# A mixture-of-experts gather of 96 partitions issued over 128, with the slots of a tile laid in blocks of 32 over both halves of the partitions

## The chip, the core and the metric

The kernel runs on one NeuronCore of a Trainium2 chip. The metric is the device time of one execution in microseconds; the time before is the median of three runs. The engines named below are TensorE (PE), VectorE (DVE), ScalarE (ACT), GpSimd (POOL) and SyncE (SP). SP issues the loads of the weights, ACT issues stores, POOL issues gathers (indirect DMAs); all of them are carried out by the core's 16 DMA engines. Everything is float32.

## The reference

Two layers of a diffusion trunk over 256 latent and 256 context tokens of width 1024. A layer is a mixer and then a mixture of experts. What matters here is the mixture of layer 0, over all 512 tokens:

```python
g_logits = (x @ w_group).astype(jnp.float32) + b_group          # top-1 of 4 groups
...
top_p, top_i = lax.top_k(e_prob, MOE_TOP_K)                      # top-2 of the group's 4 experts
...
for e in range(MOE_EXPERTS):                                     # 16 experts, hidden width 512
    hdn = jax.nn.silu(x @ w_gate[e]) * (x @ w_up[e])
    y = y + combine[:, e:e + 1] * (hdn @ w_down[e])
```

An expert has three matrices of 2 MB. Each of the 512 tokens goes to two experts, so that 1024 rows are shared among 16 experts, 64 on average. With the reference's inputs the router (worked out from the inputs, not from a trace) gives, in the order in which the kernel takes its tiles (experts 15 to 2, then 0, then 1, whose last 10 tokens make a seventeenth, narrow tile): 86, 92, 79, 49, 87, 76, 63, 64, 15, 34, 51, 50, 81, 37, 54, 96 and 10 tokens. Layer 1 does the same for the 256 latent tokens, 32 rows to an expert on average; there the experts have 5, 30, 34, 25, 19, 34, 14, 35, 36, 59, 37, 56, 60, 39, 12 and 17 tokens.

## The kernel before

Each engine has its own hand-written program, and the programs wait for each other on semaphores. The experts of a layer are done one after the other, a tile of at most `CAP[0] = 96` token rows each in layer 0 (`CAP[1] = 64` in layer 1). A tile is called by its place e below, 0 to 16; its buffers are the pair p = e % 2.

**Weights.** SP loads blocks of 2 MB (gate, up and down of every expert, written `ring<-in_moe_w_gate` and so on in the trace) into a ring of 6 slots. `block_used` counts the blocks that PE is done with, and SP issues a load when its slot is free (L586 in the loop, L540 outside it). PE waits for a block with `pe.wait_ge(arrival(i), ...)` at the head of `gate_up` and `down`.

**Which token sits in which slot.** `router` runs on DVE. From the rank of a token among those of its expert it makes `sl`, the slot in the tile, and `tile`. For tiles 0 and 1 a quick way is taken: `first_hot` compares a row of slot numbers (`count_row`) with the places of the tokens (L2088), PE multiplies the result with the token numbers (bank `FIRST_IDX_BANK`), and DVE writes the indices `idx` (L2112). For all tiles DVE makes `slot_hot` (a comparison of `sl` with 0 to 127, L2133) and `tile_hot` (L2140, L2142), PE multiplies them (16 matmuls), and DVE writes `idx` again (L2154). A slot without a token gets an index beyond the bounds, and the gather skips it.

**Gathers.** `gather` on POOL copies one column of `idx` (L2760), and `rows_in` issues the indirect DMA (L2768 for layer 0, L2771 for layer 1): partition s of `xg` gets the row of `h2_rows` in HBM that is token idx[s], 4 KB in layer 0. In layer 1 a token takes two partitions, s and 64 + s, with 2 KB each. From tile 2 on the gather of tile e waits until DVE has turned the rows of tile e - 2 (`xgT_dve`). The first tile is turned by PE (`first_xt`, L1183), the others by DVE in blocks of 32 partitions (`do_rows_turned`, L2261).

**Products.** PE takes the slots in three groups of 32 as stationary operand against the weights (`do_product`, matmuls at L638 and L1089), then `do_down`. Nothing in them depends on which token is in which slot.

**Results.** DVE and ACT copy the down product into `yb`, and ACT stores it by two DMAs (`store_y`, L451 and L452) into `y_rows` in HBM, at row tile * 96 + slot. POOL fetches each token's two rows again by `y_gather` (L2808): four gathers of 128 rows after tile 13 is stored (`y_gathered_early`), four more after tile 14, four after tile 15. Their positions `py` come from `tile` and `sl` as well (L2146). The sum over the two experts is then added to the residual and normed, and layer 1 begins.

Of the kernel before, what the change touches and what calls it, by code (L numbers as in the profile page):

```python
# [13 lines left out]
P = 128  # L14
D = 1024
KC = D // P
NT = 4
# [146 lines left out]
def hybrid_dit(nc, A, out):  # L164
# [4 lines left out]
    with ctx:  # L169
# [123 lines left out]
        pick = hidT[:, 0, 2, :].rearrange("p (j n) -> p j n", j=NLAT)  # L293
        count_row, place = hidT[:, 0, 3, 0:CAP[0]], hidT[:, 1, 3, 0:2 * NT]
        first_hot = view(M_HID, 2, NT * CAP[0])
        key_hit = yb[:, :, 512:1024]
# [339 lines left out]
        def _(pe):  # L636
            def mm(o, l, r, start=True, stop=True):
                return nc.tensor.matmul(o, l, r, start=start, stop=stop)  # L638
# [358 lines left out]
            def rows_and_router(l):  # L997
# [59 lines left out]
                if l == 1:  # L1057
                    keep_clock(0, (512, 256))
                    pe.wait_ge(sem("h2_act"), NT + NLAT)
                    first_picked()  # L1060
                else:
                    for e in range(2):
                        pe.wait_ge(sem("picked"), e + 1)
                        for j in range(NT):
                            m = mm(ps[0:CAP[0], FIRST_IDX_BANK[e], 0:1], first_hot[:, e, j * CAP[0]:(j + 1) * CAP[0]],
                                   cst[:, C_TOK + j:C_TOK + j + 1], j == 0, j == NT - 1)
                        m.then_inc(sem("idx_ps"), 1)
                    pe.wait_ge(sem("h2_act"), NT)
                    ada_block(4, 3)
# [817 lines left out]
        def _(dve):  # L1887
# [109 lines left out]
            def router(l):  # L1997
# [33 lines left out]

                V.tensor_scalar(count_row[:, 0:CAP[l]], ps[:, 1, 384:384 + CAP[l]], 1.0, None, ALU.add)
                link(V.tensor_reduce(r("gm"), lgv[:, :, 0:4], AX_X, ALU.max))
# [52 lines left out]
                for e in range(2 - l):  # L2086
                    hot = pick if l == 1 else first_hot[:, e, :].rearrange("p (j n) -> p j n", j=NT)
                    V.tensor_tensor(hot, count_row[:, 0:cap].unsqueeze(1).to_broadcast([P, n, cap]),  # L2088
                                    place_of[:, e if l else 1 - e, :].unsqueeze(2).to_broadcast([P, n, cap]), ALU.is_equal)\
                        .then_inc(sem("picked"), 1)  # L2090
# [6 lines left out]
                if l == 0:  # L2097
# [12 lines left out]
                    for e in range(2):  # L2110
                        dve.wait_ge(sem("idx_ps"), e + 1)
                        V.tensor_scalar(idx[0:cap, e:e + 1], ps[0:cap, FIRST_IDX_BANK[e], 0:1], float(NO_TOKEN), None, ALU.add)\  # L2112
                            .then_inc(sem("idx_ready"), 1)
# [12 lines left out]
                if l == 0:  # L2126
                    V.tensor_tensor(r12("sl"), r12("sl"), r12("pb"), ALU.add)
                link(V.tensor_tensor(r12("tile"), r12("xk"), r12("ke"), ALU.add))

                th = tile_hot[:, 0:2 * n * NTL].rearrange("p (t k) -> p t k", t=2 * n)  # L2130
# [546 lines left out]
        def _(pool):  # L2677
# [74 lines left out]
            def gather(l, e, p):  # L2752
# [3 lines left out]
                if not (isinstance(e, int) and e < 2):  # L2756
                    pool.wait_ge(sem("xgT_dve"), EB[l] + e - 1 - l)
                ex = e if isinstance(e, int) else bass.ds(e, 1)
                rows = CAP[0] if l == 0 else P
                G.tensor_copy(idxc[0:rows, p:p + 1], idx[0:rows, e:e + 1] if isinstance(e, int) else idx[0:rows, ex])\  # L2760
                    .then_inc(sem("idx_col"), 1)
# [4 lines left out]
            def rows_in(l, b):  # L2766
                if l == 0:
                    return G.indirect_dma_start(xg[0:CAP[0], b, :], None, h2_rows,  # L2768
                                                bass.IndirectOffsetOnAxis(ap=idxc[0:CAP[0], b:b + 1], axis=0),
                                                bounds_check=NT * P - 1, oob_is_err=False)  # L2770
# [154 lines left out]
```

## Time and profile before

| | us |
|---|---|
| runs before, median of 3 | 1002.42 |
| lowest and highest of the 3 | 1001.57 and 1005.04 |
| the profiled execution, its own time | 999.99 |
| its span, from the first to the last instruction | 998.2 |
| PE busy | 944.5 (95%) |
| DVE busy | 622.6 (62%) |
| ACT busy | 182.3 (18%) |
| POOL busy | 116.2 (12%) |

The span is what the trace shows; 1.8 us of the execution's own time lie around it. A busy PE is not a PE at its peak, and a short wait in it can be the whole of what a transfer costs. Layer 0's mixture runs from about 315 to 625 us of the span, layer 1's from about 760 us to the end.

### The profile page before, as it was taken

The numbers are of one execution on the slowest core, as the hardware profiler recorded it, in microseconds if no ns is written. First come the engines' busy times: TensorE is split into PE (matmuls) and PEld (weight loads), VectorE is DVE, ScalarE is ACT, GpSimd is POOL, SyncE is SP. The second block draws the span as 40 slices with busy tenths as digits, with TensorE's granted clock in tenths as the row PEclk, the third lists the DMA queues.
The fourth block names the chain that finished last, engine by engine and source line by source line (L and its number), as shares of the span: only waits on it lengthen the run. The fifth ranks groups of instructions, "written<-read, shape, count | busy, mean of one in ns | idle before, by whom it ended". The sixth has DMA issues, their size and how long they took to land.

```text
span 998.2 us, 19918 instructions
## 1 busy us (share of the span) xinstructions
PE 944.5 (95%) x8010; PEld 569.0 (57%) x8010; DVE 622.6 (62%) x1527; ACT 182.3 (18%) x343; POOL 116.2 (12%) x176
## 2 busy tenths in 40 slices
PE   5999999999998999999999998999998899999986
PEld 2443433456445788988888894445644455555542
DVE  2100799879546696676866645647416977777763
ACT  3010022255024010000000003317503100000001
POOL 7010100101400200000001214100010100000000
PEclk9999999999999699999999999999999999999998
DMA  9999967456836899999999967945125899999993
GB/s 315 372 417 414 373 232 273 140 200 254 237 120 238 291 361 346 399 410 415 402 410 398 425 264 276 367 166 197 62 88 193 316 428 423 427 424 427 426 427 153
DMA packets 55758, 312.01 MB, mean 313 GB/s; under 512 B 7137, under 2 KB 17121, under 8 KB 38288
## 3 DMA queue, kind: packets, MB, share of 16 engines
q1 hardware_dynamic: 41152, 277.88, 70.3%
q0 software_dynamic: 9376, 21.20, 6.7%
q10 hardware_dynamic: 5168, 12.06, 3.2%
q8 instruction: 45, 0.74, 0.3%
q14 instruction: 17, 0.14, 0.0%
HBM read 300.52 MB, written 17.25 MB: 318 GB/s over the span
## 4 chain that ended last, share of the span: by engine, by line
PE 78%; DMA 9%; DVE 7%; issue 2%; ACT 1%; POOL 1%; SPq 1%; ACTq 0%; POOLq 0%; DVEq 0%
PE ps L638 52%; PE ps L1089 10%; DMA ring<-in_moe_w_gate 5%; PE ps L653 3%; PE ps L982 3%; PE ps L1222 2%; PE ps L1132 2%; DMA ring<-in_ada_w 2%; DMA ar<-y_rows,sm 1%; PE ps L1477 1%; DMA y_rows<-ar 1%; SPq L536 1%; PE ps L918 1%; PE ps L663 1%; PE ps L1446 1%
## 5 line engine op out<-in xcount | busy, mean ns | idle before, releaser
L638 PE MATMUL ps<-ring,ar 128*32 128x384 f32 (+6 forms) x3872 | 475.1, 464 | 7.8 <-DMA ring<-in_moe_w_gate 4.6
L638 PEld LDWEIGHTS ps<-ring,ar 128*32 128x32 f32 (+2 forms) x3872 | 196.1, 120 | 133.0 <-issue 75.2
L1089 PE MATMUL ps<-ring,ar 128*32 128x128 f32 x1488 | 167.4, 275 | 0.0
L1089 PEld LDWEIGHTS ps<-ring,ar 128*32 128x32 f32 x1488 | 163.8, 111 | 2.8
L2261 DVE STREAM_TRANSPOSE ar<-ar 32x256 f32<-32x256 f32 x304 | 132.3, 435 | 4.5
L638 PE MATMUL ps<-xh,ring 128*128 128x512 f32 x256 | 114.0, 598 | 1.4 <-ACT xh L1526 1.4
L2303 DVE TENSOR_TENSOR ar<-ar,ps 128x384 f32<-128x384 f32 (+2 forms) x33 | 15.9, 482 | 119.4 <-PE ps L1089 68.2
L638 PE MATMUL ps<-ring,xh 128*128 128x512 f32 x192 | 86.3, 605 | 2.3 <-ACT xh L1537 1.4
L638 PEld LDWEIGHTS ps<-xh,ring 128*128 128x128 f32 x256 | 47.5, 190 | 62.6 <-issue 60.4
L2432 DVE SCALAR_TENSOR_TENSOR ar<-ar,cpar 128x512 f32<-128x512 f32 x120 | 79.6, 747 | 0.0
L1597 ACT ACTIVATE ar<-ps 128x384 f32<-128x384 f32 (+2 forms) x33 | 14.3, 432 | 275.7 <-PE ps L638 192.0
L638 PEld LDWEIGHTS ps<-ring,xh 128*128 128x128 f32 x192 | 36.4, 193 | 49.0 <-issue 45.2
L2290 DVE STREAM_TRANSPOSE ar<-ar 32x64 f32<-32x64 f32 x256 | 60.5, 236 | 4.5
L2282 DVE STREAM_TRANSPOSE ar<-ar 32x128 f32<-32x128 f32 x144 | 59.5, 413 | 2.9
L1132 PE MATMUL ps<-ring,ar 128*32 128x256 f32 x256 | 57.9, 379 | 0.0
L2760 POOL COPY sm<-sm 96x1 int32 (+3 forms) x32 | 6.0, 189 | 325.1 <-DVE ar L2261 309.6
L653 PE MATMUL ps<-ring,silu_c 128*32 128x512 f32 x320 | 40.1, 619 | 0.0
L2400 DVE TENSOR_TENSOR ar<-ps,gm 128x512 f32<-128x512 f32 x12 | 8.3, 690 | 50.8 <-PE ps L638 39.7
L1132 PEld LDWEIGHTS ps<-ring,ar 128*32 128x32 f32 x256 | 28.1, 110 | 18.0
L1602 ACT ACTIVATE ar<-ps 128x512 f32<-128x512 f32 x16 | 9.6, 598 | 150.2 <-PE ps L638 150.2
L2421 DVE TENSOR_TENSOR ar<-ps,ar 128x512 f32<-128x512 f32 x4 | 2.8, 693 | 43.5 <-PE ps L638 43.5
L1222 PE MATMUL ps<-ar 64*128 64x512 f32 x120 | 29.8, 615 | 0.0
(398 smaller groups left out, 946.6 us busy)
## 6 DMA issues: line engine op xcount, KB each, us to landing
ring<-in_moe_w_gate SPq DMA_DIRECT2D x31, 2048.0 KB, 16.4
ring<-in_moe_w_up SPq DMA_DIRECT2D x30, 2048.0 KB, 15.6
ring<-in_moe_w_down SPq DMA_DIRECT2D x30, 2048.0 KB, 17.8
ring<-in_ada_w SPq DMA_DIRECT2D x24, 2048.0 KB, 13.6
ring<-in_even_w_in SPq DMA_DIRECT2D x4, 2048.0 KB, 14.8
y_rows<-ar POOLq DMA_DIRECT2D x17, 384.0 KB, 10.2
ring<-in_odd_w_in SPq DMA_DIRECT2D x3, 2048.0 KB, 19.4
y_rows<-ar ACTq DMA_DIRECT2D x16, 288.0 KB, 8.9
```

Source lines behind the costliest of these rows:

```text
L638: return nc.tensor.matmul(o, l, r, start=start, stop=stop)
L653: m = nc.tensor.matmul(ps[32 * q:32 * q + 32, LATE_BANK if g == 4 and n >= 2 else ADA_BANK[g], :], silu_c[:, 2 * k + c, 10 - 2 * s:42 - 2 ...
L982: m = nc.tensor.matmul(ps[:, j, :], mix[:, c, j * P:(j + 1) * P], blk(i)[:, c, :], start=(c == 4), stop=(c == 3), skip_group_check=True)
L1089: m = nc.tensor.matmul(ps[96:128, bank, g * P:(g + 1) * P], xgT[:, p, c, 32 * g:32 * g + 32], w[:, c, 3 * P:HID], start=c == 0 and g == 0, ...
L1132: nc.tensor.matmul(ps[96:128, 5, 256 * g:256 * g + 256], tokens(g, c), w[:, c, 768:D], start=c == 0 and g == 0, stop=c == HC - 1 and g == ...
L1222: m = nc.tensor.matmul(acc(j, h), mixw[64 * h:64 * h + 64, p, j * P:(j + 1) * P], yb[64 * h:64 * h + 64, p, 0:512], start=False, stop=True ...
L1597: A_(hid[:, p, 0:hw], ps[:, 0, 0:hw], ACT.Silu).then_inc(sem("silu_done"), 1)
L2261: m = V.transpose(xgT[32 * q:32 * q + 32, p, :, slots], rows)
L2282: V.transpose(hidT[32 * q:32 * q + 32, p, :, 32 * r:32 * r + 32], cols[:, q, :, :])
L2290: m = V.transpose(hidT[32 * q:32 * q + 32, p, 0:2, 32 * r:32 * r + 32], cols[:, q, :, :])
L2303: V.tensor_tensor(hid[:, p, 0:hw], hid[:, p, 0:hw], ps[:, 1, 0:hw], ALU.mult).then_inc(sem("hid_ready"), 1)
L2432: V.scalar_tensor_tensor(acc[n], u_in[:, n, :, bass.ds(t, 256)], cpar[:, n, bass.ds(t, 1)], acc[n], ALU.mult, ALU.add).then_inc(sem("conv_ ...
```

## The change

Layer 0's gathers are issued over all 128 partitions of `xg` instead of 96. Slots 0 to 31 stay on partitions 0 to 31, slots 32 to 63 go to partitions 64 to 95, slots 64 to 95 to partitions 32 to 63; the last 32 partitions have no token and are skipped. For tiles 0 and 1 the new order comes from a permuted `count_row`, with `first_hot` 128 instead of 96 wide; for the others from four more DVE operations on `sl` (add 32 from slot 32 on, take 64 away from slot 64 on). `py` follows `sl`, so the rows of `y_rows` are permuted within a tile too.

```diff
@@ -291,8 +291,8 @@
         slot_of, half_of = (tile_hot[:, half + NTL + k:half + NTL + k + 1] for k in (8, 9))
         mixw = hid[:, :, 256:512]
         pick = hidT[:, 0, 2, :].rearrange("p (j n) -> p j n", j=NLAT)
-        count_row, place = hidT[:, 0, 3, 0:CAP[0]], hidT[:, 1, 3, 0:2 * NT]
-        first_hot = view(M_HID, 2, NT * CAP[0])
+        count_row, place = hidT[:, 0, 3, :], hidT[:, 1, 3, 0:2 * NT]
+        first_hot = view(M_HID, 2, NT * P)
         key_hit = yb[:, :, 512:1024]
         posy, posy_early = sm[:, 16:24].bitcast(I32), sm[:, 8:16].bitcast(I32)
         EARLY = NEXP - 2
@@ -1062,7 +1062,7 @@
                     for e in range(2):
                         pe.wait_ge(sem("picked"), e + 1)
                         for j in range(NT):
-                            m = mm(ps[0:CAP[0], FIRST_IDX_BANK[e], 0:1], first_hot[:, e, j * CAP[0]:(j + 1) * CAP[0]],
+                            m = mm(ps[:, FIRST_IDX_BANK[e], 0:1], first_hot[:, e, j * P:(j + 1) * P],
                                    cst[:, C_TOK + j:C_TOK + j + 1], j == 0, j == NT - 1)
                         m.then_inc(sem("idx_ps"), 1)
                     pe.wait_ge(sem("h2_act"), NT)
@@ -2029,7 +2029,9 @@
                 link(V.tensor_tensor(lgv, ps[:, 1, 0:32 * n].rearrange("p (j k) -> p j k", k=32)[:, :, 0:20],
                                      r_bias.unsqueeze(1).to_broadcast([P, n, 20]), ALU.add))
 
-                V.tensor_scalar(count_row[:, 0:CAP[l]], ps[:, 1, 384:384 + CAP[l]], 1.0, None, ALU.add)
+                V.tensor_scalar(count_row[:, :].rearrange("p (a b s) -> p a b s", a=2, b=2) if l == 0 else count_row[:, 0:CAP[1]],
+                                ps[:, 1, 384:512].rearrange("p (b a s) -> p a b s", a=2, b=2) if l == 0
+                                else ps[:, 1, 384:384 + CAP[1]], 1.0, None, ALU.add)
                 link(V.tensor_reduce(r("gm"), lgv[:, :, 0:4], AX_X, ALU.max))
                 V.tensor_tensor(r4("ge"), lgv[:, :, 0:4], b4("gm"), ALU.subtract).then_inc(sem("g_shift"), 1)
                 link(V.tensor_tensor(r4("eq"), lgv[:, :, 0:4], b4("gm"), ALU.is_equal))
@@ -2085,8 +2087,9 @@
                                             ALU.add, ALU.mult))
                 for e in range(2 - l):
                     hot = pick if l == 1 else first_hot[:, e, :].rearrange("p (j n) -> p j n", j=NT)
-                    V.tensor_tensor(hot, count_row[:, 0:cap].unsqueeze(1).to_broadcast([P, n, cap]),
-                                    place_of[:, e if l else 1 - e, :].unsqueeze(2).to_broadcast([P, n, cap]), ALU.is_equal)\
+                    wide = CAP[1] if l else P
+                    V.tensor_tensor(hot, count_row[:, 0:wide].unsqueeze(1).to_broadcast([P, n, wide]),
+                                    place_of[:, e if l else 1 - e, :].unsqueeze(2).to_broadcast([P, n, wide]), ALU.is_equal)\
                         .then_inc(sem("picked"), 1)
                 ranks = ranks.unsqueeze(1).to_broadcast([P, 2, n, 16])
                 V.tensor_tensor(r32("t12"), r32("M12"), ranks, ALU.mult)
@@ -2109,7 +2112,7 @@
                                            ALU.mult, ALU.add)
                     for e in range(2):
                         dve.wait_ge(sem("idx_ps"), e + 1)
-                        V.tensor_scalar(idx[0:cap, e:e + 1], ps[0:cap, FIRST_IDX_BANK[e], 0:1], float(NO_TOKEN), None, ALU.add)\
+                        V.tensor_scalar(idx[:, e:e + 1], ps[:, FIRST_IDX_BANK[e], 0:1], float(NO_TOKEN), None, ALU.add)\
                             .then_inc(sem("idx_ready"), 1)
 
                 V.tensor_tensor(r32("t12"), r32("lower"), over_experts(nov), ALU.mult)
@@ -2124,8 +2127,13 @@
                 link(V.tensor_tensor(r12("xk"), r12("xk"), r12("ne"), ALU.add))
                 link(V.scalar_tensor_tensor(r12("xk"), r12("kk"), 0.0, r12("xk"), ALU.is_gt, ALU.mult))
                 if l == 0:
-                    V.tensor_tensor(r12("sl"), r12("sl"), r12("pb"), ALU.add)
+                    link(V.tensor_tensor(r12("sl"), r12("sl"), r12("pb"), ALU.add))
                 link(V.tensor_tensor(r12("tile"), r12("xk"), r12("ke"), ALU.add))
+                if l == 0:
+                    V.tensor_scalar(r12("pb"), r12("sl"), 32.0, 32.0, ALU.is_ge, ALU.mult)
+                    link(V.tensor_scalar(r12("q"), r12("sl"), 64.0, -64.0, ALU.is_ge, ALU.mult))
+                    link(V.tensor_tensor(r12("pb"), r12("pb"), r12("q"), ALU.add))
+                    link(V.tensor_tensor(r12("sl"), r12("sl"), r12("pb"), ALU.add))
 
                 th = tile_hot[:, 0:2 * n * NTL].rearrange("p (t k) -> p t k", t=2 * n)
                 th4 = tile_hot[:, 0:2 * n * NTL].rearrange("p (k j t) -> p k j t", k=2, t=NTL)
@@ -2756,8 +2764,7 @@
                 if not (isinstance(e, int) and e < 2):
                     pool.wait_ge(sem("xgT_dve"), EB[l] + e - 1 - l)
                 ex = e if isinstance(e, int) else bass.ds(e, 1)
-                rows = CAP[0] if l == 0 else P
-                G.tensor_copy(idxc[0:rows, p:p + 1], idx[0:rows, e:e + 1] if isinstance(e, int) else idx[0:rows, ex])\
+                G.tensor_copy(idxc[:, p:p + 1], idx[:, e:e + 1] if isinstance(e, int) else idx[:, ex])\
                     .then_inc(sem("idx_col"), 1)
                 pool.wait_ge(sem("idx_col"), EB[l] + e + 1 - l)
                 pool.sem_inc(sem("waits_passed"), 1)
@@ -2765,8 +2772,8 @@
 
             def rows_in(l, b):
                 if l == 0:
-                    return G.indirect_dma_start(xg[0:CAP[0], b, :], None, h2_rows,
-                                                bass.IndirectOffsetOnAxis(ap=idxc[0:CAP[0], b:b + 1], axis=0),
+                    return G.indirect_dma_start(xg[:, b, :], None, h2_rows,
+                                                bass.IndirectOffsetOnAxis(ap=idxc[:, b:b + 1], axis=0),
                                                 bounds_check=NT * P - 1, oob_is_err=False)
                 return G.indirect_dma_start(xg[:, b, 0:512], None, h2_halves,
                                             bass.IndirectOffsetOnAxis(ap=idxc[:, b:b + 1], axis=0),
```

On DVE, in layer 0's `router`, between the last sums that give slot and tile and the comparison that makes `slot_hot` (128x1024), there stood before (all names are of the one buffer `ar`; `ps` is PSUM):

```order
L2125 SCALAR_TENSOR_TENSOR ar<-ar 128x8 [waits dve_chain]
L2127 TENSOR_TENSOR ar<-ar 128x8 [waits dve_chain]
L2128 TENSOR_TENSOR ar<-ar 128x8
L2133 TENSOR_TENSOR ar<-ps,ar 128x1024 [waits dve_chain]
L2140 TENSOR_TENSOR ar<-ps,ar 128x256
L2142 TENSOR_TENSOR ar<-ar,cst 128x256 [waits dve_chain]
```

At the same place of the changed kernel (its lines are numbered 8 higher from here on):

```order
L2130 TENSOR_TENSOR ar<-ar 128x8 [waits dve_chain]
L2131 TENSOR_TENSOR ar<-ar 128x8 [waits dve_chain]
L2133 TENSOR_SCALAR ar<-ar 128x8 [waits dve_chain]
L2134 TENSOR_SCALAR ar<-ar 128x8
L2135 TENSOR_TENSOR ar<-ar 128x8 [waits dve_chain]
L2136 TENSOR_TENSOR ar<-ar 128x8 [waits dve_chain]
L2141 TENSOR_TENSOR ar<-ps,ar 128x1024 [waits dve_chain]
L2148 TENSOR_TENSOR ar<-ps,ar 128x256
L2150 TENSOR_TENSOR ar<-ar,cst 128x256 [waits dve_chain]
```

Four operations of 8 elements have come in, three of them waiting for the one before, and one wait more stands ahead of the sum for `tile` (L2131). The two comparisons for tiles 0 and 1, further ahead on DVE, are 128x512 instead of 128x384.

On POOL, at the start of layer 0's dispatch, the clearing of `xg`, and the first two gathers before:

```order
L2747 MEMSET ar 128x2048 [waits chosen,y_zero]
L2760 COPY sm<-sm 96x1 [waits h2_stored0,h2_stored1,idx_ready,pool_chain]
L2768 DMA ar<-h_rows,sm 96x1024 [waits idx_col]
L2760 COPY sm<-sm 96x1 [waits idx_ready]
L2768 DMA ar<-h_rows,sm 96x1024 [waits idx_col]
```

and of the changed kernel:

```order
L2755 MEMSET ar 128x2048 [waits chosen,y_zero]
L2767 COPY sm<-sm 128x1 [waits h2_stored0,h2_stored1,idx_ready,pool_chain]
L2775 DMA ar<-h_rows,sm 128x1024 [waits idx_col]
L2767 COPY sm<-sm 128x1 [waits idx_ready]
L2775 DMA ar<-h_rows,sm 128x1024 [waits idx_col]
```

No order and no wait has moved there; the copy and the gather are wider. PE, ACT and SP keep their rows, but for the 8 one-column matmuls of tiles 0 and 1, which give 128 rows instead of 96.

## Rows read from the trace of the kernel before

**Rows 1.** The page: the chain that ended last, share of the span by engine.
```profile
PE 78%; DMA 9%; DVE 7%; issue 2%; ACT 1%; POOL 1%; SPq 1%; ACTq 0%; POOLq 0%; DVEq 0%
```

**Rows 2.** Windows of layer 0's tiles: us, busy time, PEclk, DMA share, GB/s.
```profile
381.70:397.40 15.70, 15.70 (x270) 13.48 (x264) 11.07 (x27) 1.09 (x2) 1.15 (x2) 1.00 0.90 326
...
444.30:538.30 94.00, 93.69 (x1578) 80.64 (x1571) 65.58 (x157) 6.52 (x12) 6.95 (x12) 1.00 1.01 406
```

**Rows 3.** Waits between 320 and 620 us: total, times, longest.
```profile
PE ps L638 <- DMA ring<-in_moe_w_gate: 2.1, 1, 2.1
...
PE ps L638 <- DMA ring<-in_moe_w_down: 0.3, 1, 0.3
```

**Rows 4.** The chain that ended last, 500 to 630 us: start, us, what.
```profile
514.21 28.37 DMA ring<-in_moe_w_gate
...
591.27 7.25 DMA y_rows<-ar
...
599.31 0.99 POOL xh L2808
...
613.37 10.49 DMA ar<-y_rows,sm
```

**Rows 5.** Layer 0's last two weight loads: SP's timeline, and their landing.
```profile
558.84 5.57 SPq L540 DMA_DIRECT2D ring<-in_moe_w_down  x2
...
DMA to landing us min/median/max: 25.1/25.3/25.4
```

**Rows 6.** Windows at the end of layer 0's and of layer 1's weights (columns as rows 2).
```profile
568.00:576.00 8.00, 8.00 (x130) 6.03 (x129) 6.42 (x16) 0.60 (x1) 2.84 (x2) 1.00 1.01 423
576.00:580.00 4.00, 4.00 (x81) 4.00 (x74) 1.11 (x3) 0.39 (x1) 0.00 (x0) 1.00 0.98 416
580.00:584.00 4.00, 4.00 (x82) 4.00 (x74) 0.00 (x0) 0.10 (x1) 0.00 (x0) 1.00 0.73 304
584.00:589.20 5.20, 5.20 (x81) 4.33 (x76) 4.14 (x10) 0.00 (x0) 0.23 (x1) 1.00 0.32 130
976.00:980.00 4.00, 3.70 (x26) 1.59 (x24) 2.08 (x9) 0.00 (x0) 0.00 (x0) 1.00 0.88 354
980.00:983.00 3.00, 2.35 (x12) 0.63 (x10) 2.86 (x11) 0.00 (x0) 0.00 (x0) 1.00 0.19 78
```

**Rows 7.** DVE's timeline in layer 0's router.
```profile
322.13 1.03 DVE L2088 TENSOR_TENSOR ar<-ar 128x384 f32<-128x384 f32 x2
...
327.56 0.17 DVE L2125 SCALAR_TENSOR_TENSOR ar<-ar 128x8 f32<-128x8 f32 x1
327.76 0.17 DVE L2127 TENSOR_TENSOR ar<-ar 128x8 f32<-128x8 f32 x1
327.85 0.16 DVE L2128 TENSOR_TENSOR ar<-ar 128x8 f32<-128x8 f32 x1
328.04 1.23 DVE L2133 TENSOR_TENSOR ar<-ps,ar 128x1024 f32<-128x1024 f32 x1
```

**Rows 8.** PE's timeline there; idle time before it and its releaser in brackets.
```profile
330.11 3.62 PE L638 MATMUL ps<-ar 128*128 128x32 f32 x16 [1.08 <-DVE ar L2142]
333.55 1.52 PE L1183 MATMUL ps<-cst,ar 96*128 96x96 f32 x8
```

**Rows 9.** Layer 0's first gather, the landing of its 17, and layer 1's gathers (128 wide).
```profile
327.62 1.03 POOL L2768 DMA_INDIRECT ar<-h_rows,sm  x1 [0.98 <-POOL sm L2760]
...
DMA to landing us min/median/max: 4.6/10.4/10.9
...
L2771 POOL DMA_INDIRECT ar<-h_rows,sm x15: 1013/1019/1077, 776.7 to 933.4; - x15
```

**Rows 10.** Window about the first tile (columns as rows 2).
```profile
330.00:340.70 10.70, 9.80 (x71) 9.01 (x75) 5.16 (x27) 1.77 (x2) 2.07 (x3) 0.50 1.02 354
```

**Rows 11.** The second store of tile 13 and the first early gather: timelines of ACT and POOL.
```profile
575.70 0.45 ACTq L452 DMA_DIRECT2D y_rows<-ar  x1
...
588.97 1.09 POOL L2808 DMA_INDIRECT xh<-y_rows,sm  x1 [18.07 <-DMA y_rows<-ar]
```

## Prediction

> **What bounds the kernel now.** I read the page first. The chain that ended last is PE for 78% of the span and DMA for 9% [rows 1], so anything done to a gather counts only where PE stands still for it, where its transfer is itself on the chain, or where it takes DMA time from what is. The second view is the windows over layer 0's tiles. Tile after tile PE is busy 15.7 of 15.7 us, while the 16 DMA engines are busy too: the share is 0.90 about tiles 2 and 3 and 1.01 from tile 6 to 12 [rows 2]. Two resources are nearly even here, and a few tenths of a microsecond per tile decide which is ahead. The third view says who is: of 320 to 620 us PE waits once for a gate block, 2.1 us, and once for a down block, 0.3 us [rows 3]. The chain has the first of them: a gate block is issued at 514.21 and lands 28.37 us later, at 542.58, where PE had arrived at 542.58 - 2.1 = 540.5 [rows 4]. For twelve tiles PE has lived on the lead of the ring, and at 540 it is used up.
>
> The fourth view shows what kind of lateness that is. The last load of layer 0 is issued at 558.84 + 5.57 - 0.33 = 564.1 and lands 25.1 us later, at 589.2 [rows 5]. All 16 engines should be busy until then. They are not: the share is 0.98, then 0.73, then 0.32 in the last 5.2 us [rows 6]. Some engines have done their part long before the slowest, and a block counts as landed only when the slowest has. The unused engine time is 4 x 0.02 + 4 x 0.27 + 5.2 x 0.68 = 4.7 us per engine: the slowest engine is 4.7 us behind the mean. The weight blocks are alike for all engines, so it is the rows of the gathers (4 KB, whole rows per engine) that are laid unevenly. At the end of layer 1, whose gathers fill both halves of the partitions, the same sum is 4 x 0.12 + 3 x 0.81 = 2.9 us [rows 6].
>
> **What the change does to the DMA engines.** At 423 GB/s over 16 engines [rows 6] a row of 4 KB costs an engine 4096 / 26,400 = 0.155 us. Backlog builds up from tile 6 on (before it the share is below 1, and a light engine simply idles). Tiles 6 to 15 have 63, 64, 15, 34, 51, 50, 81, 37, 54 and 96 tokens, 545 in all, 34 per engine. Two ways of dealing partitions to engines fit the 4.7 us of before. (a) Eight engines serve partitions 0 to 63, each two blocks of four (0-3 and 32-35, and so on), eight serve 64 to 127: the heaviest gets 8 rows of a tile of 64, in sum 74, that is 40 above the mean or 6.2 us. (b) Consecutive partitions, six per engine: the heaviest gets 60, 26 above, 4.0 us. Layer 1 tells them apart for gathers of 128: with its tokens on s and 64 + s, in rows of 2 KB (0.078 us), (a) gives a heaviest engine of 95 rows against a mean of 64, 2.4 us; eight consecutive partitions per engine give 125 rows, 4.7 us. Measured are 2.9, nearer to (a). I take (a). After the change slots 0 to 31 then fall on the first eight engines, 32 to 63 on the other eight, and only tokens beyond 64 go back to the first: the heaviest engine gets 4 rows of a tile, 8 of one above 67, in sum 48, 14 above the mean or 2.2 us. So the slowest engine is earlier at 542 by 4.7 - 2.2 = 2.5 us, by (a) alone 26 x 0.155 = 4.0 us. I take 3, and keep 0.8 as the lower bound: layer 1's 2.9 us over 15 tiles of half-size rows, scaled to 10 tiles of whole ones, is 3.9 us, only 0.8 less than 4.7.
>
> The Trainium skill says the same of the deal in "DMA: Bandwidth & Descriptors", section "The descriptor swizzle": a 128-partition transfer is dealt by fours, engines 0 to 7 for partitions 0 to 63. By that rule, the trace of layer 1 agrees (2.9 us beside 2.4). The same page, section "Why a DMA increments its semaphore by 16 and not by 1", speaks against the change: it counts a 96-partition tile among those that use all 16 engines, six partitions each. By that reading before is case (b), 60 rows against 48 after: 12 x 0.155 = 1.9 us instead of 3, and PE would still wait a few tenths.
>
> **What it costs ahead of the first tile.** Four operations of 8 elements come in on DVE ahead of the comparison for `slot_hot`, and one wait more. A pair with a wait between is 0.20 us apart, one without 0.09 (327.56, 327.76, 327.85) [rows 7]: 3 x 0.20 + 0.09 for the four, and 0.11 for the wait, 0.8 us. The two comparisons of tiles 0 and 1 go from 384 to 512 columns: they take 0.52 each, and 1024 columns 1.23, so 1.1 ns a column, 2 x 128 x 1.1 = 0.28 us [rows 7]. Together 1.1 us. This lies on the chain: PE waits 1.08 us for L2142 before the 16 index matmuls at 330.11, and runs the first tile's turn right behind them at 333.7 [rows 8]. The first gather stays covered: issued at 327.62, landed 4.6 us later at 332.2, 1.5 us before it is needed [rows 9]; it moves by only the 0.28. POOL's issue of a gather costs 1.03 us and a 128-wide one of layer 1 1.019, nothing to add [rows 9]. PE's granted clock is 0.50 through 330 to 340.7 [rows 10]; 1.1 us of delay can cost between 0.6 (the clock rises at the same moment, and the work pushed behind it runs at twice the rate) and 2.6 (it rises some 3 us late). I take 1.1. Later gathers have a whole tile of 15.7 us for landings of 10.4 [rows 2, 9], and DVE, busy 11 of 15.7, turns blocks of 32 partitions as before.
>
> **The sum.** PE arrives at the critical block at 540.5 + 1.1 - 0.3 (the down wait, gone) = 541.3. The block, pushed by 1.1 as well since its stream is paced by PE until about tile 6, lands at 542.58 + 1.1 - 3 = 540.7. The wait is gone, and PE goes on at 541.3 instead of 542.6: -1.3 us. What follows runs at PE's pace: per tile the heaviest engine has 6.3 MB / 16 of weights, a store of 0.39 MB / 16 and 4.8 rows, 0.44 MB at 26.4 GB/s, 16.6 us, where before it had 7.4 rows and 17.0; that is more than 15.7, so a little of the gain is eaten again, but only three tiles are left.
>
> At the end of the layer the stores are on the chain. POOL's first early gather starts at 588.97, when tile 13's store has landed, 13.3 us after its issue at 575.70 [rows 11]: that store shares the engines with the last weights, and the slowest engine is the one that holds 4.7 us more. Even engines end at 589.2 - 2.5 = 586.7 or before, so the four early gathers (1.3 us apart) start 1 to 2.5 us earlier, and tile 14's store, issued at 591.27 in the midst of them and landed 7.25 us later [rows 4], meets less of them. POOL's next gathers (599.31) wait for it. Beyond the 1.3 us that everything moves I count 1.0 more here (bounds 0 and 3). From there to the end all is released by layer 0's results, and moves along. Sum: -1.3 - 1.0 = -2.3 us on the profiled execution, 999.99 to 997.7. The runs lie higher (median 1002.42); the same difference gives 1000.1.
>
> **Rivals.** (A) As above: -2.3 us, for itself -3.5 to -1.0. Chance 0.40. (B) The wait is not removed: before is even enough (case (b), or the bound of 0.8 us). Then the block lands at 542.58 + 1.1 - 0.8 = 542.9, PE goes on 0.3 later, and the tail brings nothing: 1002.7. For it speaks that layer 1 in both halves still ends 2.9 us uneven, and (A) with a late clock (+1.5) comes to the same, -0.8. Chance 0.27. (C) On the other side: the gather of 128 is dealt in consecutive eights. Then real rows sit on engines 0 to 3 and 8 to 11, the heaviest takes 80 rows for 74 or 60 before, 0.9 to 3.1 us more; the block lands at 544.6 to 546.8, PE waits 3 to 5 us, and the last weights end as much later: +2 to +5 us, 1005.5. It decides from the point at which the heaviest engine has over 2 rows a tile more than before. Against it stands layer 1's 2.9 us where it would be 4.7. Chance 0.13. (D) The tail brings all of its 3 us, or the runs without a profile wait longer for weights than the 2.1 us here (they are 2.4 us longer): -4 to -6 us, 997.4. Chance 0.20.
>
> **How the numbers follow.** 0.3% is 3.0 us, about what a measurement of this kernel tells from no change. Faster by more: (D), and 0.16 of (A), whose end reaches there: 0.36. Slower by more: (C) mostly and a little of (B): 0.15. The rest, 0.49, is within. The range goes from (D)'s 996.0 to the near half of (C), 1004.0.
>
> **What would show it.** The gate wait of 2.1 us at 542 is gone, or it is not, and then (B) or (C); the share of the DMA engines near the end of layer 0's weights falls within 2 to 3 us instead of over 11; L2142's successor releases PE 1.1 us later (a wait of about 2.2 in place of 1.08); the first early gather starts before 588. The prediction is wrong if the unevenness is not that of the gathers, if the clock stays low longer, or if faster engines start the layer's last transfers into each other.

## The result and the profile after

The changed kernel takes 998.12 us (median of 12 runs, 994.9 to 1001.97) beside 1004.17 for the kernel before in the same session (1000.73 to 1007.89): a ratio of 0.9944, 95% interval 0.9925 to 0.9964, so 5.6 us faster (the two medians by themselves lie 6.05 apart). Its profiled execution takes 996.33 us, span 994.4, 3.7 us less than that of before. The forecast was 2.3 us and a range of 996 to 1004: the side and the range are right, the size is more than twice what was said (on the profiled execution 3.7 for 2.3), and the reason, as the experiments show, is another.

Windows of the kernel after (columns as [rows 2]); the first two answer to [rows 2], the next four to [rows 6], the last to [rows 10]:

```profile
381.70:397.40 15.70, 15.70 (x272) 13.52 (x268) 11.07 (x27) 1.09 (x2) 1.19 (x2) 1.00 0.90 342
444.30:538.30 94.00, 94.00 (x1590) 80.90 (x1585) 65.73 (x157) 6.52 (x12) 7.16 (x12) 1.00 1.01 427
568.00:576.00 8.00, 8.00 (x146) 6.73 (x142) 5.59 (x14) 0.60 (x1) 3.14 (x2) 1.00 0.92 381
576.00:580.00 4.00, 4.00 (x79) 4.00 (x74) 0.00 (x0) 0.49 (x1) 0.45 (x1) 1.00 0.14 52
580.00:584.00 4.00, 4.00 (x61) 2.86 (x54) 0.71 (x2) 0.00 (x0) 3.09 (x4) 1.00 0.60 145
584.00:589.20 5.20, 5.07 (x103) 3.11 (x100) 4.94 (x13) 0.60 (x1) 0.55 (x1) 1.00 0.66 238
330.00:340.70 10.70, 8.53 (x80) 7.40 (x80) 6.99 (x31) 1.77 (x2) 2.22 (x3) 0.66 0.92 339
```

What strikes is the second row. The engines are as busy as before (share 1.01) and move 427 GB/s where it was 406. With all engines busy in both kernels, a fairer deal of the rows among them does not explain a higher sum. The layer's last weight lands at 578.1 instead of 589.2 (the share is 0.14 from 576 to 580; what follows at 580 are the early gathers), 11.1 us earlier where the forecast said 2.5. PE no longer waits for a weight block anywhere from 320 to 620 us; its waits there (answering to [rows 3]):

```profile
PE ps L1053 <- DVE ar L2068: 1.9, 1, 1.9
PE ps L638 <- DVE ar L2150: 1.4, 1, 1.4
PE ps L638 <- DVE ar L2091: 1.1, 1, 1.1
PE ps L638 <- issue: 0.8, 1, 0.8
```

Windows of 5 us show where the rate was lost. The kernel before, then after:

```profile
515.00:520.00 5.00, 5.00 (x92) 4.65 (x87) 0.75 (x2) 0.00 (x0) 1.16 (x2) 1.00 1.02 430
520.00:525.00 5.00, 5.00 (x83) 3.25 (x75) 4.85 (x13) 0.52 (x1) 0.00 (x0) 1.00 1.05 368
```

```profile
520.00:525.00 5.00, 5.00 (x83) 3.31 (x79) 4.83 (x13) 0.60 (x1) 0.00 (x0) 1.00 1.04 437
```

The stretch at 368 GB/s is the one in which a gather's rows move. In the window of after a gather's rows move too, from 520 to 523. The trace's records of single packets say it more sharply (starts within each us; mean duration of the 16 KB weight packets of all engines, share of them over 0.63 us, rows of 4 KB):

```
before  519: 0.611 us  0.00   0 rows      after  519: 0.611 us  0.00   0 rows
        521: 0.796     1.00  12                  520: 0.611     0.00  20
        522: 0.766     1.00  11                  521: 0.611     0.00  21
        523: 0.762     1.00  10                  522: 0.612     0.00  12
        526: 0.617     0.08   0                  523: 0.616     0.00   1
```

Before, while rows move, a weight packet takes 0.70 to 0.80 us on average instead of 0.61, and none is spared (a share of 1.00, so on all engines, whatever rows they carry); the rows themselves drip in over 5 us rather than 3. After, nothing of it is left. Over 444.3 to 538.3 a weight packet takes 0.646 us on average before and 0.613 after: (0.646 - 0.613) x 2099 packets / 16 = 4.3 us per engine.

### The profile page after: what moved, and what is told of

Same layout as the page of the kernel before. It is cut to its first block, busy times and chain, and to the rows that moved or that the text cites. A ratio compares the mean times of both kernels' runs of the same rounds, so it can differ in the third digit from the quotient of the medians.

```text
span 994.4 us, 19922 instructions
## 1 busy us (share of the span) xinstructions
PE 943.2 (95%) x8010; PEld 564.1 (57%) x8010; DVE 623.3 (63%) x1531; ACT 182.0 (18%) x343; POOL 116.9 (12%) x176
## 4 chain that ended last, share of the span: by engine, by line
PE 79%; DVE 8%; DMA 6%; issue 2%; another core or an unknown queue 2%; ACT 1%; SPq 1%; POOL 0%; ACTq 0%; DVEq 0%; POOLq 0%
PE ps L638 52%; PE ps L1089 11%; PE ps L653 3%; PE ps L982 3%; DMA ring<-in_moe_w_gate 3%; PE ps L1132 3%; PE ps L1222 3%; DMA ring<-in_ada_w 2%; DMA ar<-y_rows,sm 1%; PE ps L1477 1%; SPq L536 1%; PE ps L918 1%; DVE ar L2290 1%; PE ps L663 1%
## 5 line engine op out<-in xcount | busy, mean ns | idle before, releaser
L638 PEld LDWEIGHTS ps<-ring,ar 128*32 128x32 f32 (+2 forms) x3872 | 188.1, 120 | 132.3 <-issue 74.1
L2767 POOL COPY sm<-sm 128x1 int32 (+1 forms) x32 | 5.9, 185 | 324.4 <-DVE ar L2269 309.2
## 6 DMA issues: line engine op xcount, KB each, us to landing
ring<-in_moe_w_up SPq DMA_DIRECT2D x30, 2048.0 KB, 12.9
```

## The experiments

Two parts of the change could do that: the placement (P) or the width of the gather (W). Two kernels took them apart, each timed beside the one before.

**Slots left in place, gather 128 wide.** The changed kernel with

```
-  ps[:, 1, 384:512].rearrange("p (b a s) -> p a b s", a=2, b=2) if l == 0
+  ps[:, 1, 384:512].rearrange("p (a b s) -> p a b s", a=2, b=2) if l == 0
-  V.tensor_scalar(r12("pb"), r12("sl"), 32.0, 32.0, ALU.is_ge, ALU.mult)
+  V.tensor_scalar(r12("pb"), r12("sl"), 512.0, 32.0, ALU.is_ge, ALU.mult)
-  ... V.tensor_scalar(r12("q"), r12("sl"), 64.0, -64.0, ALU.is_ge, ALU.mult)
+  ... V.tensor_scalar(r12("q"), r12("sl"), 512.0, -64.0, ALU.is_ge, ALU.mult)
```

> The changed kernel with its slots left where they were (0 to 95 in order; the iota row is not permuted and the two thresholds are set so high that nothing is added), everything else kept: the gather over 128 partitions, the 4 added VectorE operations, the wide comparisons. The traces show that of before's weight stream all 16 engines ran slow (368 GB/s over 520 to 525 us, 426 elsewhere) just while a gather's rows moved, and of after's none did (422 to 431). Theory P (placement: it is the uneven share of the engines' rows that slows them): as before, 365 to 385 GB/s in those stretches, layer 0's last weight lands near 589, time 1.000 to 1.003 of before. Theory W (width: a gather over 96 partitions slows all engines, one over 128 doesn't): no stretch under 420, last landing 580 to 583, PE's wait for the gate block gone, time 0.995 to 0.998 of before.

Measured: 998.0 us, ratio 0.9929 (0.9901 to 0.9957).

**Slots spread, gather 96 wide.** The changed kernel with

```
-  return G.indirect_dma_start(xg[:, b, :], None, h2_rows,
+  return G.indirect_dma_start(xg[0:CAP[0], b, :], None, h2_rows,
-      bass.IndirectOffsetOnAxis(ap=idxc[:, b:b + 1], axis=0),
+      bass.IndirectOffsetOnAxis(ap=idxc[0:CAP[0], b:b + 1], axis=0),
```

> The changed kernel with only the gather's width taken back: slots spread as in it (they lie in partitions 0 to 95), gathered over 96 partitions rather than 128. P: as the changed kernel, 0.993 to 0.996 of before, 422 to 431 GB/s throughout. W: slow stretches while rows move (365 to 385 GB/s), last landing 583 to 586, 0.997 to 1.000 of before. A third theory C (rows dealt to the engines by consecutive partitions, six each for 96 of them, not in blocks of four): the spread loses its point as well, time 1.000 or above.

Measured: 1005.38 us, ratio 0.9997 (0.9972 to 1.0021).

Windows of the first kernel (in place), then windows and PE's wait of the second:

```profile
444.30:538.30 94.00, 94.00 (x1592) 80.90 (x1584) 65.73 (x157) 6.53 (x12) 7.18 (x12) 1.00 1.01 427
520.00:525.00 5.00, 5.00 (x84) 3.26 (x79) 4.82 (x13) 0.60 (x1) 0.00 (x0) 1.00 1.03 432
```

```profile
444.30:538.30 94.00, 93.79 (x1581) 80.86 (x1573) 65.71 (x157) 6.52 (x12) 6.96 (x12) 1.00 1.01 401
520.00:525.00 5.00, 5.00 (x88) 3.36 (x78) 4.83 (x13) 0.60 (x1) 0.00 (x0) 1.00 1.04 359
```

```profile
PE ps L638 <- DMA ring<-in_moe_w_gate: 1.9, 1, 1.9
```

So the gather's width carries the whole gain, and the placement adds none that can be measured. W's time for the first (0.995 to 0.998) was even too cautious. A block's landing has 16 records in the trace, and they give the lag of the last engine behind the first, for the block that lands at about 542: before 13.5 us, spread and 96 wide 11.7, in place and 128 wide 11.4, changed 5.5. So the spread does even out the engines, but only in a 128-wide gather, and the kernel with 11.4 us of lag is as fast as that with 5.5. The layer's last weight shows both parts: it lands at 589.2 before, at 588.7 spread and 96 wide (W had said 583 to 586), at 582.5 in place and 128 wide, and at 578.1 in the changed kernel. Some 7 of the 11.1 us are the width's, some 4 the spread's, and these 4 bring no time that shows.

**The spread made elsewhere, without the router's added operations.** The list of indices is permuted as it is written, and the transposes read the blocks back (the edits that widen the gathers are left out here):

```
+  PLACES = [(b, (0, 2, 1, 3)[b], slice(2, NTL)) for b in range(4)]
...
-  V.tensor_scalar(idx[:, 2:NTL], ps[:, IDX_BANK[0], 2:NTL], float(NO_TOKEN), None, ALU.add)
+  for to, at_, cols in PLACES:
+      m = V.tensor_scalar(idx[32 * to:32 * to + 32, cols], ps[32 * at_:32 * at_ + 32, IDX_BANK[0], cols], ...
...
-  rows = xg[slots, p, :].rearrange("s (c q i) -> s q c i", c=KC, q=4)[:, q, :, :]
+  rows = xg[at_, p, :].rearrange("s (c q i) -> s q c i", c=KC, q=4)[:, q, :, :]
```

> The kernel before, with the spread made in another place: slots keep their order everywhere but in the rows gathered for tiles 2 to 16, whose list of indices is written to partition blocks 0, 2, 1, 3 by four small VectorE operations in place of one; the transposes read the blocks back in order. Gathers 128 wide from tile 2 on, 96 wide and in place for tiles 0 and 1. None of the 4 operations and wide comparisons ahead of the first tile. By the prediction's price of these (1.1 us) 1 us faster than the changed kernel, 0.992 to 0.995 of before. If that price was hidden (the clock gave it back in the profiled run), the same as the changed kernel.

> As the last, and in odd tiles the two halves of the partitions change places (slots 0 to 31 in partitions 64 to 95, 32 to 63 in 0 to 31, 64 to 95 in 96 to 127), at 4 more small VectorE operations. Heaviest engine of layer 0: 82 rows rather than 96, mean 64. If the distance between first and last engine follows the rows at 0.155 us, it falls from some 5 us to some 3. If PE alone sets the pace once the stream is ahead of it, the time is that of the last within 0.3% (1 us more if the added operations show). If the stream still sets it, 1 to 2 us faster than that.

Measured: 996.6 us, 0.9893 (0.9853 to 0.9933), and with the halves of odd tiles exchanged (four more such operations) 998.55, 0.9927 (0.9906 to 0.9948). Both move 427 GB/s in 444.3 to 538.3, and neither can be told from the others that are 128 wide. The exchange was to bring the lag of the engines from some 5 us to some 3; it was 4.4 us instead of 5.9 at the block that lands at 541 and 5.8 instead of 5.9 at the layer's last, so that expectation did not hold.

The next four kernels ask for the smallest change that does it, what width it takes, whether it takes rows, and what delays the layer's end.

**Width only, 128 and 112; gathers held; no rows.** To the kernel before:

```
-  rows = CAP[0] if l == 0 else P
+  rows = CAP[0] if l == 0 and isinstance(e, int) and e < 2 else P        (in the second, 112 in layer 0)
-  return G.indirect_dma_start(xg[0:CAP[0], b, :], None, h2_rows,
+  return G.indirect_dma_start(xg[0:rows, b, :], None, h2_rows,
...
```

> The kernel before with one thing changed: the gathers of tiles 2 to 16 go over 128 partitions, the last 32 skipped; slots, VectorE's work and the gathers of tiles 0 and 1 as before. W (the width is all that counts): 422 GB/s or more in every stretch from 444 to 538, PE's wait for the gate block gone, 0.989 to 0.995 of before, as fast as the changed kernel or 1 us faster (the router's added operations are gone). P (placement counts as well): above the changed kernel by 1 us or more.

> As the kernel of width only, with 112 partitions in place of 128. If any width beyond 96 does, or if it is the blocks of six partitions that are slow: as the kernel of 128. If the width has to be a full 128 (seven partitions per engine are dealt as unevenly as six): slow stretches (under 390 GB/s over 5 us) while rows move, 0.997 to 1.001 of before.

> The kernel before, gathers 96 wide and issued as before, but with the bound of their indices at 0 for tiles 2 to 16, so that they leave all rows but token 0's out (those tiles compute on what lies in the buffer; the output is not the reference's). If it is the moving rows that slow the weights: no stretch under 420 GB/s, first to last engine within 2 us, last weight of layer 0 landing at 574 to 577, and a time within 0.3% of the changed kernel if PE alone sets it there. If the issue of a 96-partition gather slows them without rows: stretches under 400 GB/s stay.

> As the last, and GpSimd waits with the early gathers of the stored rows until TensorE is through with the down block of tile 14 (they were issued from 579.6 us on in the changed kernel and from 589.0 in the one before). Theory I: in the changed kernel these gathers move while instructions are fetched (packets of the instruction queue start at 586.5 there, at 582.8 if the pattern of before held), which costs tile 14 the 1.4 us by which its output is late; held back, tile 14's output follows tile 13's by 15.7 us again (17.0 in the changed kernel), and layer 0 ends 1 to 2 us earlier than in the last. Theory N: the loss has another cause, tile 14 stays late, the time is that of the last or up to 2 us longer.

Width only: 1000.21 us, 0.9939 (0.9906 to 0.9972): the changed kernel's gain with nothing else of it. 112 wide: 1003.77 us, 0.998 (0.9946 to 1.0015), with the slow stretches of 96 and the gate wait (2.3 us). The kernel of no rows leaves out the gathered rows, so that layer 1 gets other numbers to route by, and its 1030.93 us, ratio 1.027, say nothing; what layer 0 does can be read. It has no slow stretch, so the slowing takes moving rows, and the lag between the engines is 2.8 us. The output of tile 13 comes at 570.12 in it, and at 570.20 in the kernel of width only, at the same granted clock (0.68 over 330 to 340.7): with 128 partitions the rows cost PE nothing any more. Windows of width only, then of 112 wide, then of no rows:

```profile
444.30:538.30 94.00, 94.00 (x1592) 80.95 (x1588) 65.86 (x157) 6.52 (x12) 7.17 (x12) 1.00 1.01 427
520.00:525.00 5.00, 5.00 (x91) 3.73 (x84) 4.83 (x13) 0.60 (x1) 0.00 (x0) 1.00 1.04 436
```

```profile
444.30:538.30 94.00, 93.53 (x1574) 80.45 (x1568) 65.38 (x156) 6.52 (x12) 7.11 (x12) 1.00 1.01 405
520.00:525.00 5.00, 5.00 (x83) 3.21 (x72) 4.85 (x13) 0.56 (x1) 0.00 (x0) 1.00 1.04 368
```

```profile
444.30:538.30 94.00, 94.00 (x1592) 80.93 (x1588) 65.76 (x157) 6.54 (x12) 6.97 (x12) 1.00 1.01 428
```

The gathers held back concern another place. In the changed kernel tile 14's output comes 17.0 us after tile 13's, where the tiles before it are 15.6 to 15.7 apart, and tile 15's comes 11.6 us after that, for 8.7 before. ACT's output copies of tiles 13, 14 and 15:

```profile
571.11 0.60 ACT L1602 ACTIVATE ar<-ps 128x512 f32<-128x512 f32 x1 [9.93 <-PE ps L638]
...
588.15 0.60 ACT L1602 ACTIVATE ar<-ps 128x512 f32<-128x512 f32 x1 [11.31 <-PE ps L638]
...
599.75 0.60 ACT L1602 ACTIVATE ar<-ps 128x512 f32<-128x512 f32 x1 [9.37 <-remote]
```

Held (`pool.wait_ge(sem("block_used"), at["d", 0, NEXP - 2] + 1)` ahead of the early gathers, in the kernel of width only): 1000.1 us, 0.9958 (0.9931 to 0.9985). Tile 14 follows tile 13 by 15.66 us, as theory I wanted, and then tile 15 by 15.2 instead of 10.2: the loss has moved, and grown by 3.5 us. PE's timeline and windows there:

```profile
590.25 0.42 PE L638 MATMUL ps<-ring,ar 128*32 128x128 f32 x5 [0.29 <-issue]
590.97 0.42 PE L638 MATMUL ps<-ring,ar 128*32 128x128 f32 x4 [0.29 <-issue]
591.69 0.45 PE L638 MATMUL ps<-ring,ar 128*32 128x128 f32 x5 [0.30 <-issue]
```

```profile
590.00:592.00 2.00, 1.15 (x14) 0.51 (x15) 0.00 (x0) 0.28 (x1) 1.61 (x2) 1.00 0.78 170
594.00:596.00 2.00, 2.00 (x26) 1.62 (x29) 0.72 (x3) 0.00 (x0) 0.00 (x0) 0.50 0.99 375
```

TensorE runs four to six small matmuls and then waits 0.29 us for nothing that the profile shows, six times in the 4 us from 590 to 594. The granted clock is at the lower level (0.50, 1.2 GHz) right behind it, in 594 to 596. That one does not always follow the other: the 112-wide kernel and the spread, 96-wide one have six such pauses between 591 and 595.5 too, and keep the full clock until past 600.

The last four ask whether the loss comes from the rows of the early gathers and whether 64 does what 128 does, and run two kernels once more. The edit of the first, to the kernel of width only:

```
-  y_gather(j, posy_early, sem(f"yg_in{j}"))
+  y_gather(j, posy_early, sem(f"yg_in{j}"), 0)      (the bound of its indices)
```

> The kernel of width only, whose early gathers of stored rows are issued but bring none (the bound of their indices is 0; the rows of tiles 0 to 13 are left out of the sum for two of the token blocks, so that layer 1 routes otherwise and the time as a whole says nothing). Read from 560 to 603 us. In the runs so far the outputs of tiles 14 and 15 came 15.7 + 8.7 us after that of tile 13 (before), 17.0 + 11.6 (changed), 17.1 + 10.2 (width only), 15.7 + 15.2 (width only, gathers held to 588.2). Theory I (the rows of these gathers hold up what TensorE and its neighbours fetch): 15.7 + 8.7 or less. Theory N (another cause): 17 + 10 as before.

> As the kernel of width only, with 64 partitions: rows of slots 64 to 95 are left out (those tiles compute on what lies there; layer 1 routes otherwise, so only layer 0 is read). 96 and 112 partitions slowed all weight packets while rows moved (368 GB/s), 128 didn't. If it takes the full 128: slow stretches (under 400 GB/s in some 5 us of each tile). If it takes a power of two, or a multiple of 64: none, 422 or more throughout.

> The kernel that turns the spread rows back in the transposes, which had 0.989 of before (0.985 to 0.993), once more, beside the changed kernel: if the router's added operations cost their 1.1 us, it is 1 us or more under the changed kernel; if the clock pays for them, both are within 0.3% of each other.

> The changed kernel once more, for the comparison with the last on one chip: 0.9925 to 0.9964 of before.

Without the early rows (994.44 us in its one run) tiles 14 and 15 come 17.1 and 10.2 us after each other, to a tenth as in the kernel of width only. Theory I falls: it is not the rows of these gathers that hold PE up. 64 wide (1011.15 us in one run; PE waits 7.0 us for its first tile's rows, and slots beyond 64 are left out; layer 0's rates alone are read) is slow as well: 403 GB/s over the six tiles from 444 to 538, and, where rows move,

```profile
510.00:514.00 4.00, 4.00 (x59) 2.46 (x57) 3.25 (x8) 0.00 (x0) 0.00 (x0) 1.00 1.03 384
...
527.00:531.00 4.00, 4.00 (x66) 2.29 (x58) 3.88 (x11) 0.00 (x0) 0.00 (x0) 1.00 1.03 337
```

Of 64, 96, 112 and 128 partitions only 128 is free of it. The kernel with the blocks turned back had 997.68 us, 0.9928 (0.989 to 0.9965), the changed one beside it 998.75, 0.9926 (0.9897 to 0.9955): the same ratio. The medians are 1.07 us apart, which neither shows nor excludes the 1.1 us of the router's added operations. The version that looked best at first does not beat the changed kernel by anything that can be measured. DVE's and PE's timelines in the router of this second execution of the changed kernel answer to [rows 7, 8]:

```profile
329.18 1.22 DVE L2141 TENSOR_TENSOR ar<-ps,ar 128x1024 f32<-128x1024 f32 x1
```

```profile
331.25 3.62 PE L638 MATMUL ps<-ar 128*128 128x32 f32 x16 [1.39 <-DVE ar L2150]
334.68 1.52 PE L1183 MATMUL ps<-cst,ar 96*128 96x96 f32 x8
336.99 0.85 PE L638 MATMUL ps<-ring,ar 128*32 128x384 f32 x2 [0.78 <-DVE ar L2259]
```

Here the clock is at 0.50, as before, and all of it stands 1.1 us later than in [rows 7, 8] (329.18 for 328.04, 334.68 for 333.55). In the first execution the 16 matmuls already ran at the level of 2.4 GHz:

```profile
331.64 1.97 PE L638 MATMUL ps<-ar 128*128 128x32 f32 x16 [1.39 <-DVE ar L2150]
333.45 1.12 PE L1183 MATMUL ps<-cst,ar 96*128 96x96 f32 x8
```

1.97 us instead of 3.62, which hid the cost. The kernel of width only, without these operations, had that early clock too in its profile, so it is not the change that brings it.

The times at which tiles 13 and 15 are put out (ACT's copies) gather most of this; "clock" is the granted one over 330 to 340.7:

```
                                width  clock  tile 13   tile 15   between
before                             96   0.50   574.37    598.70     24.3
spread                             96   0.68   573.60    602.12     28.5
112 wide                          112   0.51   574.89    604.14     29.3
changed                           128   0.66   571.11    599.75     28.6
changed, again                    128   0.50   572.20    600.12     27.9
in place                          128   0.66   571.16    599.02     27.9
turned back (two executions)      128   0.50   571.53    599.51     28.0
                                  128   0.50   571.31    598.36     27.1
turned back, odd tiles exchanged  128   0.50   571.75    600.21     28.5
width only                        128   0.68   570.20    597.51     27.3
width only, held                  128   0.50   571.63    602.46     30.8
width only, no early rows         128   0.68   570.15    597.43     27.3
```

Where the early gathers start matters to which tile is late. In the eight kernels and executions in which they start between 579.5 and 583.6, tile 14 comes 16.2 to 18.4 us after tile 13 and tile 15 another 9.5 to 11.9. In the held, the 112-wide and the spread, 96-wide kernel, in which they start between 588.2 and 589.7, tile 14 comes after 15.7 to 16.1 and tile 15 after another 12.9 to 15.2. Before starts them at 588.97 too and has neither delay, so their start alone is not the cause.

## Why the prediction was right in its range and wrong in its reason

**What bounds the kernel: right.** PE was just ahead of the weights, and the two block waits of [rows 3] are gone in every kernel whose gathers are 128 wide. At one clock (0.50) tile 13 is put out at 574.37 before and at 571.3 to 571.75 in the 128-wide kernels without the router's operations: 2.6 to 3.1 us, where the forecast counted 2.1 + 0.3.

**"I take (a)": the step that failed.** The forecast asked only which engines carry the rows, took fours also for the 96-wide gather, and made the spread the cause. In place and 128 wide has the full gain (0.9929), spread and 96 wide has none (0.9997). The deal itself comes out as two. For 128 partitions the spread takes the lag from 11.4 to 5.5 us, as a deal by fours would (15.2 and 7.0, worked out from the rows of tiles 0 to 12 at 0.155 us) and one by consecutive eights would not (16.1 for both). For 96 the spread hardly helps (11.7 for 13.5); six consecutive partitions per engine would give 11.0 and 11.8, and by fours 7.0 would be left (the consecutive deal was theory C of the second experiment, whose time, 1.000 or above, is within the interval measured). The other widths bear this out: consecutive partitions give some 13.5 us for 112 (measured 14.1) and 4.8 for 64 (3.4 and 3.8), where fours would leave over 14 for 64. The Trainium skill's page "DMA: Bandwidth & Descriptors", section "Why a DMA increments its semaphore by 16 and not by 1", counts a 96-partition tile among those on all 16 engines, and the forecast weighed that reading, six partitions each, and passed it over. By that reading, the traces agree (11.7 and 13.5 beside 11.0 and 11.8). It would still not have given the gain: in place and 128 wide PE waits for no block, with a lag of 11.4 us.

**"So the slowest engine is earlier by ... I take 3": mis-sized, for a term left out.** The sum priced rows alone, 0.155 us each, and left the weight packets at one price throughout. The runs show the packets of the whole core at 0.68 to 0.80 us instead of 0.61 for 4 to 5 us of every tile from 444 to 538, 4.3 us per engine over six tiles, and the layer's last weight 7 to 9 us earlier with the width alone (582.5 in place, 580.4 width only), 11 with the spread. 368 GB/s beside 430 stood in the trace of before: six windows of 5 us would have shown that the loss comes with the gathers and strikes all engines, which no uneven deal explains. The predicted mark, a share of the engines that falls within 2 to 3 us at the end of the weights instead of over 11, was not met: the last block's first part lands at 572.2 and its last at 578.1, 5.9 us (before 578.3 and 589.2).

**The cost ahead of the first tile: right.** Predicted 1.1 us, measured 1.1 at one clock. By tile 13 it is 0.6 to 1.0 (572.20 beside 571.53, 571.31 and 571.63; 571.11 and 571.16 beside 570.20 with the early clock). The predicted mark, a wait of 2.2 us behind L2142 (now L2150), was wrong: PE came later as well, behind its earlier work, and waited 1.39.

**The tail: the mark right, the gain not.** The first early gather starts at 579.55, 9.4 us earlier (forecast: before 588). But tile 14's store is issued only 1.7 us earlier (589.54 for 591.27), since PE lost 1.4 us on tile 14 and 2.9 on tile 15. The chain that ended last, after (answers to [rows 4]; the program runs on one core, so the two lines of "another core or an unknown queue" are stretches for which the profile names no releaser):

```profile
573.89 9.28 another core or an unknown queue
...
590.14 9.59 another core or an unknown queue
...
600.74 5.02 DMA y_rows<-ar
...
611.53 10.59 DMA ar<-y_rows,sm
```

The table shows that this loss does not come with the width: the 96- and 112-wide kernels have it too, and only the one profiled execution of before lacks it (24.3 us from tile 13 to 15, all others 27 to 31). That execution, at 999.99 us, was also faster than all 12 runs of before in the session of the result (1000.73 to 1007.89). So the two profiles probably understate the gain, and the runs are the ones to believe; whether the other executions of before have the loss, no profile shows.

**The rivals.** (A), the forecast, had its wait removed by the part of the change that it had counted at nothing, the width ("nothing to add"), so the right side and range are luck. (B) and (C) fell with the gate wait. The size, -5.6 us, is that of (D), whose second half said that runs without a profile wait longer; nothing here shows what they wait for.

**What stays open.** Why a gather over fewer than 128 partitions slows the weights' packets on every engine. The deal changes with the width as well (fours for 128, consecutive partitions for 64, 96 and 112), and no run parts the two. What PE waits for after its loop of tiles: not the early rows, and not the time of their issue alone. And where the gain comes from beyond the 2 to 3 us that the profiles show by tile 13: spread and 96 wide to changed is one edit, worth 2.8 us in the spans (997.2 to 994.4) and 0.53% in the runs.

## What to carry to other kernels

When an indirect gather runs beside a stream of loads that fills the DMA engines, look at the GB/s of short windows with and without moving rows before thinking of which engine carries what: busy share 1.0 does not say that the engines move what they can. Here the cure was to issue the gather over all 128 partitions and let the unused ones be skipped, at no cost that showed. And split a change that does two things at once: here the half that had the argument brought no time.

## What the runs showed of the hardware

- An indirect gather of 4 KB rows over 64, 96 or 112 partitions slowed the 16 KB packets of another queue while its rows moved: from 0.61 us to 0.66 to 0.82 on average within a microsecond for 96 and 112, and to 0.69 to 0.93 for 64 (337 to 384 GB/s in the windows shown, for 430 to 437). Over 128 partitions, the same rows did not (427 to 428 GB/s over six tiles). A 96-wide gather that brought no rows didn't either.
- 32 skipped partitions more cost nothing visible: POOL's issue took 1.01 us, and each skipped partition seems to leave a packet of 4 bytes on the gathers' queue, of 9 ns: from 320 to 592 us there are 978 before and 1459 in the kernel of width only with the gathers held, 481 more for 15 x 32 = 480 more skipped partitions. (The changed kernel has 1648, with early gathers in the same stretch.)
- A lag of 11.4 us between first and last engine cost PE nothing as long as the slowest engine was ahead of it.
- Six pauses of TensorE (0.29 us each, over 4 us) between groups of four to six small matmuls were followed by the lower clock in one execution (0.50 in 594 to 596) and by none in two others.
